# State-space coefficients among the input projections, a new layout of the first stage, and X by token tile

## The reference

```
proj = rms_norm(h, norm1_g) @ w_in            # q 512, k and v 256, u 512 columns
attn = sliding_window_attention(q, k, v)      # window 128, meta tokens always visible
# state space: 32 groups, 16 channels, 64 complex states each
dt = exp(log_dt);  abar = exp(lr*dt) * (cos(li*dt) + i sin(li*dt))
coef = (abar - 1) / (lr + i li);  bbar = coef * b
s_t = abar * s_{t-1} + bbar @ u_t             # associative scan over the tokens
y = Re(c @ s) + d * u;  ssm = glu(gelu(y))
h = h + concat(rms_norm(attn), rms_norm(ssm)) @ w_out
```

## Time and profile before

| | us |
|---|---|
| median of 3 runs (lowest, highest) | 4692.57 (4691.49, 4697.60) |
| the profiled execution | 4690.48 |
| its span, first to last instruction | 4689.0 |
| busy: PE, DVE, ACT, POOL | 4133.8, 2447.1, 1351.7, 24.6 |
| `First` ends and its w_out projection begins on PE | 421.4 |
| mean granted clock of PE (1 is 2.4 GHz) | 0.919 |

### The profile page before, as it was taken

The page is one execution under the profiler, slowest core; times in us unless marked ns, Lnnn a source line. Parts: engine busy times, 40 slices in busy tenths (PEclk is TensorE's granted clock), DMA queues, the critical chain, the costliest instruction groups (busy, mean ns, idle before and its releaser), DMA issues.

```text
span 4689.0 us, 46819 instructions
## 1 busy us (share of the span) xinstructions
PE 4133.8 (88%) x19069; PEld 3239.9 (69%) x19069; DVE 2447.1 (52%) x3968; ACT 1351.7 (29%) x2067; POOL 24.6 (1%) x40
## 2 busy tenths in 40 slices
PE   7347999999999999998999765899999987579999
PEld 6345888666677888887877554788778775357877
DVE  3773788777734444443332876433233239764331
ACT  3124322333333333332222222322132232223221
POOL 0000000000000000000000000000000000000000
PEclk9568999999999999998999876899999998768999
DMA  3001245455566666652332110133322321101232
GB/s 94 9 1 45 81 134 142 150 180 180 179 196 188 188 186 188 195 177 75 95 97 74 54 56 0 41 94 95 99 72 95 96 71 41 51 1 59 94 99 68
DMA packets 253286, 473.52 MB, mean 101 GB/s; under 512 B 15808, under 2 KB 138848, under 8 KB 250896
## 3 DMA queue, kind: packets, MB, share of 16 engines
q1 hardware_dynamic: 253072, 470.53, 33.0%
HBM read 399.95 MB, written 70.52 MB: 100 GB/s over the span
## 4 chain that ended last, share of the span: by engine, by line
PE 77%; DVE 17%; ACT 4%; issue 1%; DMA 0%; POOL 0%; DVEq 0%; ACTq 0%; SPq 0%; POOLq 0%
PE ps L353 23%; PE ps L355 22%; PE ps L354 22%; DVE arena L1111 2%; PE ps L456 2%; DVE arena L1718 2%; DVE arena L2568 1%; DVE st L2566 1%; PE ps L2117 1%; PE ps L2093 1%; DVE arena L2485 1%; DVE wtwo L344 1%; DVE arena L1714 1%; DVE arena L1715 1%; PE ps L1567 1%
## 5 line engine op out<-in xcount | busy, mean ns | idle before, releaser
L344 DVE TENSOR_TENSOR wtwo<-wraw,wtwo 128x1024 fp32r<-128x1024 f32 x416 | 507.8, 1224 | 828.9 <-ACT wtwo L334 828.6
L353 PE MATMUL ps<-XH,wtwo 128*128 128x512 f32 (+1 forms) x1928 | 790.6, 410 | 2.6 <-DVE wtwo L344 2.6
L355 PE MATMUL ps<-XH,wtwo 128*128 128x512 f32 (+1 forms) x1928 | 759.8, 394 | 0.0
L354 PE MATMUL ps<-XL,wtwo 128*128 128x512 f32 (+1 forms) x1928 | 759.5, 394 | 0.0
L334 ACT ACTIVATE wtwo<-wraw 128x1024 fp32r<-128x1024 f32 x416 | 437.8, 1056 | 463.1 <-PE ps L355 442.3
L344 DVE TENSOR_TENSOR wlast<-wraw,wlast 128x1024 fp32r<-128x1024 f32 x202 | 246.8, 1224 | 427.4 <-ACT wlast L334 427.2
L355 PEld LDWEIGHTS ps<-XH,wtwo 128*128 128x128 f32 x1928 | 363.2, 188 | 86.6
L353 PEld LDWEIGHTS ps<-XH,wtwo 128*128 128x128 f32 x1928 | 364.2, 189 | 76.0 <-issue 5.4
L354 PEld LDWEIGHTS ps<-XL,wtwo 128*128 128x128 f32 x1928 | 364.7, 189 | 70.3
L353 PE MATMUL ps<-XH,wlast 128*128 128x512 f32 x920 | 379.7, 413 | 2.6 <-DVE wlast L344 2.6
L355 PE MATMUL ps<-XH,wlast 128*128 128x512 f32 x920 | 364.8, 397 | 0.0
(11 more groups left out here) (418 smaller groups left out, 6548.0 us busy)
## 6 DMA issues: line engine op xcount, KB each, us to landing
wraw<-in_ut SPq DMA_DIRECT2D x128, 512.0 KB, 4.2
wraw<-in_v SPq DMA_DIRECT2D x128, 512.0 KB, 4.1
wraw<-in_ffn_gate SPq DMA_DIRECT2D x88, 512.0 KB, 3.5
wraw<-in_ffn_up SPq DMA_DIRECT2D x88, 512.0 KB, 3.5
wraw<-in_ffn_down SPq DMA_DIRECT2D x88, 512.0 KB, 3.5
acts<-arena SPq DMA_DIRECT2D x128, 256.0 KB, 4.5
gates<-arena SPq DMA_DIRECT2D x16, 2048.0 KB, 9.1
arena<-gates SPq DMA_DIRECT2D x32, 1024.0 KB, 7.9
```

The lines of the kernel that those rows point to most:

```text
L344: ve.e.tensor_tensor(W.items[n][8], W.rawof(n), W.items[n][7], ALU.subtract).then_inc(*ve.up("wlo", n))
L353: mm(out, lh, rh, start=start, stop=False)
L354: mm(out, lh, rl, start=False, stop=False)
L355: return mm(out, ll, rh, start=False, stop=stop)
```

## The change

1. The coefficients leave the merged part. `ac_coef` stands ahead of ACT's squares. `ve_coef` is a generator of 15 pieces, and `ve_in` takes two of them ahead of the norm and three after each split of q's blocks, of kv's blocks and of u's blocks, as long as there are any. The merged part has 15 state-space steps fewer on every engine.
2. X comes in four DMAs, one for each token tile, and ACT's square of a tile waits for that tile alone. The DMA of `rows` goes behind the first three weight blocks; only attention waits for it. B and C are loaded there too, where before they came after the input part.
3. Memory: the coefficients have a level of their own that lives through the input part. No places of the weights are lent. The norm's scratch lies in Q, and the meta tokens' square waits for ACT's own instruction before it. The doubling steps' scratch lies in MT. The mask MB lies in `First`, and GpSimd makes it after the setup, with the clears of `LB`, without waiting for the input part.
4. As nothing is lent, the blocks of w_out go on in the usual turn, and the fourth of them is split with u's last block instead of ahead of the merged part. The two later mixers' lendings are numbered 0 and 1 instead of 1 and 2.

```diff
@@ First.__init__
-        ar = k.level(4096 + 2112)
-        self.MT, self.XC = ar(8, 512), ar(16, 132)
+        ar = k.level(4096 + 2112 + 272)
+        self.MT, self.XC, self.MB = ar(8, 512), ar(16, 132), ar(272)
         ar = k.level(2048 + 1280)
         self.Q, self.KV = ar(4, 512), ar(5, 256)
-        ar = k.level(3072)
+        self.plan_coef(k.level(11552))
+        ar = k.level(512)
         self.XH, self.XL = k.rounded("XH", 8, 528), k.rounded("XL", 8, 528)
-        self.XMr, self.XM, self.mem = ar(1024), ar(1024), ar(1024)
...
+        self.XMr, self.XM, self.mem = Qf[:, 0:1024], Qf[:, 1024:2048], Qf[:, 1024:2048]
...
-        self.lent = k.W.lend()
-        ar = self.ar = k.level(18432)
-        self.plan_ssm()
+        self.plan_ssm(k.level(6848))
@@ order
-        na, ns = 6 + 3 + 7 * 8 + 5 + 1 + 5, 70
+        na, ns = 6 + 3 + 7 * 8 + 5 + 1 + 5, 55
@@ ac_in
-        ac.wait_ge(*at("x"))
+        self.ac_coef()
         for i in range(4):
+            ac.wait_ge(*at("x", i))
             ac_square(k, 0, i, self.mem)
@@ ve_in
+        coef = self.ve_coef()
+
+        def some(n):
+            for _ in range(n):
+                next(coef, None)
+
+        some(2)
         self.norm.ve()
-        splits(k, split_ve, "q", 512)
+        for c in range(4):
+            split_ve(k, ("q", c))
+            some(3)
         for i in (1, 3):
             ve.wait_ge(*at("tok", "q", i))
             v.tensor_copy(self.Q[:, i, :], k.got("q", i)).then_inc(*ve.free(("q", i)))
             ve.note("Q", i)
-        splits(k, split_ve, "kv", 256)
+        for c in range(2):
+            split_ve(k, ("kv", c))
+            some(3)
         for i in (1, 3):
             ve.wait_ge(*at("tok", "kv", i))
             v.tensor_copy(self.KV[:, i, :], k.got("kv", i)[:, 0:256]).then_inc(*ve.free(("kv", i)))
             ve.note("KV", i)
         for m in range(4):
             split_ve(k, ("u", m))
+            some(3)
             ve.wait_ge(*at("proj", ("u", m)))
@@ ac_ssm, now ac_coef
-        split_ac(k, 0)
         a(dt, k.col("ldt", 0, 16), ACT.Exp).then_inc(*ac.up("dt"))
         ac.wait_ge(*at("lrdt"))
         a(mag, t1, ACT.Exp).then_inc(*ac.up("mag"))
         ac.wait_ge(*at("angle"))
         a(sn, r, ACT.Sin)
         a(cs, t2, ACT.Sin).then_inc(*ac.up("cs"))
-        for _ in range(15):
-            yield
@@ po_ssm
-        k.begin(po, "in", "pe", "ac", "ve")
+        g, MB = po.e, self.MB
+        g.memset(MB, 0.0).then_inc(*po.up())
...
@@ sp
-        sp.e.dma_start(k.X[:, :, :], d["x"].rearrange("(i p) n -> p i n", p=128)).then_inc(*sp.dma("x", "x"))
+        for i in range(4):
+            sp.e.dma_start(k.X[:, i, :], d["x"][128 * i:128 * i + 128, :]).then_inc(*sp.dma(f"x{i}", "x", i))
         sp.e.dma_start(self.XMr[0:16, :], d["meta_tokens"]).then_inc(*sp.dma("meta", "meta"))
         load(k)
+        for x, n in ((self.BR, "b_re"), (self.BI, "b_im"), (self.CR, "c_re"), (self.CI, "c_im")):
+            sp.e.dma_start(x, d[n]).then_inc(*sp.dma("ssm", "ssm", n))
+        sp.e.dma_start(k.rows[:, :], d["rows"].broadcast_to([128, NROW])).then_inc(*sp.dma("rows", "rows"))
```

More of the change, by code:

```diff
@@ L502, in ac @@
             ac.wait_ge(*at("meta"))
-            a(self.XM[0:16, :], self.XMr, ACT.Square, accum_out=ss[0:16, 4:5]).then_inc(*ac.up("sqM", n))
+            ac.after().activation(self.XM[0:16, :], self.XMr, ACT.Square, accum_out=ss[0:16, 4:5]).then_inc(*ac.up("sqM", n))
         ac.wait_ge(*at("xvar", n))
@@ L531, in pe @@
         k = self.k
-        for c in ("cols", "rows", "consts"):
+        for c in ("cols", "consts"):
             k.pe.wait_ge(*k.at(c))
@@ L551, in po @@
                                  base=0, pattern=[[-1, 128]], channel_multiplier=1)
[L552 to L556, removed]
         g.memset(k.CM[:, :], 0.0).then_inc(*po.up())
@@ L686, in ve_in @@
         XCm = self.XC.rearrange("p (m j) c -> p j m c", j=4)
+        assert next(coef, "end") == "end"
         ve.wait_ge(*at("um", 3))
@@ L867, in ve_att @@
         sk = k.row("sink")
+        ve.wait_ge(*at("rows"))
         def front(n):
@@ L883, in front @@
             ve.after().tensor_tensor(l.rearrange("p (h b) n -> p h b n", b=2)[:, :, :, lo:256], local,
-                                     bc(bc(k.MB[:, lo:256], 1, 2), 1, 2),
+                                     bc(bc(self.MB[:, lo:256], 1, 2), 1, 2),
                                      ALU.add).then_inc(*ve.free(("s0", n), ("s1", n)))
-            v.tensor_tensor(l[:, :, 256:272], meta, bc(k.MB[:, 256:272], 1, 4), ALU.add).then_inc(*ve.free(("sm", n)))
+            v.tensor_tensor(l[:, :, 256:272], meta, bc(self.MB[:, 256:272], 1, 4), ALU.add).then_inc(*ve.free(("sm", n)))
             ve.after().tensor_reduce(mx, l[:, :, lo:272], AX, ALU.max).then_inc(*ve.up())
@@ L1054, in ac_ssm @@
         a = ac.e.activation
-        dt, mag, th, kk, r, s0, s1, cs, sn, ar_, ai_, den, nr, cr, ci, t1, t2, t3 = self.S[:18]
-        split_ac(k, 0)
[L1057 to L1064, removed]
         for q in range(17):
@@ L1102, in ac_ssm, with ve_tt, ve_ts, ve_times @@
         k.end("ssm", ac)
-    def ve_ssm(self):
+    def ve_tt(self, o, a, b, f):
+        self.k.ve.after().tensor_tensor(o, a, b, f).then_inc(*self.k.ve.up())
+    def ve_ts(self, o, a, x, f, y=None, f2=None):
+        ve = self.k.ve
+        if f2 is None:
+            ve.after().tensor_scalar(o, a, x, None, f).then_inc(*ve.up())
+        else:
+            ve.after().tensor_scalar(o, a, x, y, f, f2).then_inc(*ve.up())
+    def ve_times(self, outr, outi, xr, xi, sr, si):
+        tt, b3, b4 = self.ve_tt, self.b3, self.b4
+        tt(b3, xr, bc(sr, 2, 16), ALU.mult)
+        tt(b4, xi, bc(si, 2, 16), ALU.mult)
+        tt(outr, b3, b4, ALU.subtract)
+        tt(b3, xi, bc(sr, 2, 16), ALU.mult)
+        tt(b4, xr, bc(si, 2, 16), ALU.mult)
+        tt(outi, b3, b4, ALU.add)
+    def ac_coef(self):
+        k, ac, at = self.k, self.k.ac, self.k.at
+        a = ac.e.activation
+        dt, mag, th, kk, r, s0, s1, cs, sn, ar_, ai_, den, nr, cr, ci, t1, t2, t3 = self.S[:18]
+        a(dt, k.col("ldt", 0, 16), ACT.Exp).then_inc(*ac.up("dt"))
+        ac.wait_ge(*at("lrdt"))
+        a(mag, t1, ACT.Exp).then_inc(*ac.up("mag"))
+        ac.wait_ge(*at("angle"))
+        a(sn, r, ACT.Sin)
+        a(cs, t2, ACT.Sin).then_inc(*ac.up("cs"))
+    def ve_coef(self):
         k, ve, v, at = self.k, self.k.ve, self.k.ve.e, self.k.at
@@ L1373, in sp @@
             load(k, ("u", m))
-        load(k, 0)
         self.sp_ssm()
@@ L3123, in sp @@
             load(k, (key, l))
-        load(k, 1 + l)
+        load(k, l)
         self.sp_att()
```

91 lines of the change are left out of this document (41 added, 50 removed).

## The result

The changed kernel is not faster. It is 0.15% slower, within the 0.2% that the prediction calls no change. I had forecast 4662, 0.65% faster.

A forecast was written before the change was run, and what follows sets the result against it. DVE was taken to bound the merged part's coefficients (115.9 to 205.6), with room in u's projections. Projections +29.3, coefficients and q loop -82.6, outputs +5, tail +18 give -30.3: 4662 us (4652 to 4672; 8 in 10: 4644 to 4684).

The forecast's parts named there:

- The start: Load of X and squares: the meta tokens' square ends at 13.4 to 14.7 instead of 19.34; gain taken as 5.5 us.
- GpSimd's clears: Input part: two clears of 1.8 us begin near 3, end long before piece 4 of the coefficients asks; cost nothing.
- The projections: Input projections: PE stands 32 us until DVE's KV copy at 105.2; stage ends at 145.2, 29.3 later.
- rival 3: Projections of u: the clock doesn't come back after the pause; +27, so 4689, no change; chance 0.07.
- The q loop and the vector stretch: Merged part: coefficients and q loop fall from 129.1 to 46.5 us (-82.6); the vector stretch of 72.8 changes by 0.
- The outputs: Stretch 317.8 to 377.7: three attention fronts instead of two, costed by ACT's exponentials and table loads; +5 us (0 to 15).
- What the pairing gives back: Behind the last output: 15 more attention steps remain alone, one front and eight heads; +18 us (8 to 36).
- The diff touches nothing behind 421.4 us, so only this first tenth can move by itself: Premise: everything behind the first block, from 421.4 us on, keeps its length; change there 0.
- a sign of being wrong: Listed sign: any of the later stages differing by more than 5 us, for which the prediction had no mechanism.
- rivals, 1: Merged part: attention alone sets the pace, first 17 steps 69.3, tail 36; 4703, slower; chance 0.08.

The follow-up runs named there:

- e12_order68: Changed kernel with the 54 state-space steps dealt evenly over attention's first 68 steps; 4675.87 us, ratio 0.9961 to the kernel before.
- e1: Changed kernel with the count of weight places started anew at w_out's blocks, as before the change; 4697.23 us, ratio 1.0008 to the kernel before.
- e2: Changed kernel with 272 unused words per partition where the mask MB lay, restoring the addresses behind it; 4692.3 us, ratio 0.9991 to the kernel before.
- e5: Changed kernel with both the 272 unused words and the places' count restarted at w_out's blocks; 4689.7 us, ratio 0.9994 to the kernel before.
- e6: Kernel before with the places' count started anew ahead of the experts, giving the changed kernel's places from there; 4704.88 us, ratio 1.0027.
- e7: Kernel before with X in four DMAs, a wait per tile, and rows behind the first weight blocks; 4691.22 us, ratio 0.9997.
- e9 to e11: Kernel before with one, two and four DVE memsets of 1.8 us behind the last square; 4699.86, 4701.92 and 4706.39 us.
- e3: Changed kernel with the 13 later coefficient pieces spread otherwise behind the splits of q, kv and u; 4676.14 us, ratio 0.9959 to the kernel before.
- e4: Changed kernel with the 54 state-space steps dealt evenly over all 76 attention steps; 4696.32 us, ratio 1.0004 to the kernel before.
- e8: Changed kernel with 272 unused words, places' count restarted, coefficient pieces spread otherwise, and steps dealt over 68; 4646.97 us, ratio 0.9901 to the kernel before.

## Why the prediction was wrong

Forecast and profile differ by 39.0 us in the span (-30.3 against +8.7): 21.3 up to the first product with w_out, 17.7 behind it. The 21.3 are 2.2 at the end of the projections, 1.6 in the q loop, 0.8 in the vector stretch, 6.7 in the outputs, 9.7 in the tail and 0.3 behind it. So two steps failed: the pairing's cost for outputs and tail was put 16.4 too low, and the stages behind were taken as fixed, 17.7.

**The start: right in kind, 1.6 too good.** The gain is 3.9, not 5.5. The squares end at 15.36 where 13.4 to 14.7 was forecast. Row 4.61 holds it up: the operation takes 2.43 us instead of 0.17, and Sin comes at 8.83 instead of 7.0. The prediction had GpSimd's clears at nothing, and it is beside them that this operation stands (the last section has more). The table loads cost what I took: 1.28, and the activation at 3.94 follows the load of 2.65 at once. The drain that the Trainium skill's page "ScalarE: Activation LUTs", section "What ACT_TABLE_LOAD costs", adds to it isn't seen here either.

**The projections: right.** The copies that free bank 0 end at 105.7 (105.2 forecast), the pause is 32.5 (32), u's first block ends at 113.8 (113.1), the stage at 147.4 (145.2). Of the 2.2, 1.5 come behind u's first block: in the second and fourth block PE falls to the pitch of 0.43 again for 14 wide matmuls and to between 0.29 and 0.38 for four, where before it did for 8 in the third: 3.2 us of loss against 1.6. That is a small part of rival 3.

**The q loop and the vector stretch: right.** 48.1 for 46.5, and 73.6 for 72.8. The -82.6 came as -81.0.

**The outputs: +11.7 instead of +5.** ACT's busy time grew by 2.8 us, PE's by 7.3. PE's 438 matmuls were busy 51.2 us, 117 ns each, where before 452 took 43.9, 97 ns each, at a clock of 0.76 instead of 0.89: 438 x 20 = 8.8 us. I costed the third front by ACT alone and gave PE before's clock. That PE's slower matmuls are what lengthened the stretch is read from these rows; no run separates it.

**"What the pairing gives back": +27.7 instead of +18.** This is the step that failed most in the first block. I sized the 15 lone steps by bare steps of before, which ran beside the outputs at a clock of 0.89. Alone they run at 0.54, PE is busy 21.8 of 27.7, and the front's scores wait for the copy of the heads' outputs: each group of heads takes 7 to 7.7 instead of 6, the front 10.7 instead of 6. Outputs and tail together: 99.3 for 82.9, which is 16.4 of the 21.3, and e12_order68 shows that another order of the same work takes 24 off these 99.3. The forecast saw where the price would fall, but it had no row of attention alone at the low clock, and took the order as given.

**"The diff touches nothing behind 421.4 us, so only this first tenth can move by itself": +17.7.** This premise failed, and with it came a sign of being wrong that the prediction names, a later stage off by more than 5 us. 4.1 of it are the experts: addresses and places, shown by e1, e2, e5 and e6. The second layer's 3.5 are for the most part the addresses, as the pad alone takes them back (391.4, 484.6, 382.1); with the places mended beside it, in e5, mixer 1 is at 489.7. Of mixer 0's 9.6, 6.9 are the short pass that only before's profiled execution has: e7 and e9 to e11 lose it with before's memory and places, so neither is needed for the loss, and its cause is open. With the changed kernel's plan it is 489.7, 489.9 and 489.6 in three kernels (the changed one, e3, e12), 2.7 over the 487. e1 has 3.0 less and e2 2.5, but e4, which touches neither places nor addresses, 2.9, so this part isn't shown to be theirs. The change's description could have told me: part 4 moves the places, part 3 the mask. I costed both at nothing without looking behind 421.4.

Of the rivals, 1 comes nearest in its time (4703), but by luck and not by its mechanism: it put 69.3 for the first steps, where 48.1 came, and 36 for the tail, where 27.7 came. The 17.7 behind the first block were in none of them.

**Open.** What makes the clock part at 2750 us in mixer 0 (the time of entry, the place of the code, or something else), and why e4_order, with the changed kernel's plan, has 486.8 there instead of 489.7, and e5 and e8 489.7 and 489.8 in mixer 1. That the places alone cost the experts 2.6 (e2 against e5) and 3.4 (e6) is shown, by which of the shorter look-aheads isn't. That GpSimd's clears make the 2.43 us at 4.61 is argued from rows; no run moves them.

## What to carry to other kernels

Work moved into an engine's idle time costs what stands behind it in that engine's queue: here four copies, two of q and two of kv, behind fewer of the moved pieces were worth 23 us, and nothing of the moved work had to go. If one of two interleaved streams gets shorter, deal its steps over the other anew, and stop early enough for the load that waits for it: 24 us. A change of memory or of buffer phase can reach later stages that it doesn't name, and a gain of 0.2% should be compared over stages, one by one, since an edit meant as a mere delay of 1.4 us moved this kernel by 7 to 8.

## What the runs showed of the hardware

- The pitch of a matmul of 512 columns depended here on where its operands lie: 226 to 232 ns, or 233 with everything behind the mask 1088 bytes lower, restored to the nanosecond by a pad.
- The same instructions on data at the same addresses took 480.1 or 487.0 us in mixer 0, with the granted clock at 0.66 or 0.61 in a stretch of it, after an edit 2500 us earlier that only adds a clear of 1.8 us or reorders loads. Which property of the edit does it isn't shown.
- A DVE operation with one input, of 16 columns, took 2.43 us. It ended at 7.04, when GpSimd's two clears ended (3.47 + 3.54 = 7.01), while the tensor-tensor operations at 4.19 beside the same clears took their usual 0.19 each. Mixer 0 of the changed kernel has a second case: one copy of 128 columns takes 0.22 us, and 0.62 where a clear by GpSimd runs beside it, with both ends within 0.1 us of each other (2818.79 and 2818.71). Of the copy's eight occurrences only this one and its like in mixer 1 stand beside a clear, and only they are long:

```profile
2815.31 0.22 DVE L2799 COPY arena<-arena 128x128 f32<-128x128 f32 x1
...
2818.17 0.62 DVE L2799 COPY arena<-arena 128x128 f32<-128x128 f32 x1
...
2816.91 1.80 POOL L2938 MEMSET wlent<- 128x2048 f32 x1 [118.98 <-ACT wlent L2906]
```

The Trainium skill's page "GPSIMD Engine Reference", section "Specifications", says that GpSimd shares its SBUF interfaces with VectorE and contends with its instructions in a two-port mode or with two SBUF inputs. For the operations with one input the trace agrees as far as it goes, since the profile doesn't name the mode; for those with two it shows no delay.
